# Moving VectorE's share of an RWKV-7 mixer: bonus and gate, filter taps, the tail's order, and throwaway matmuls

## What is computed

```python
def mixer_ab(h, ...):
    # r, k, v, g, a, kk, decay: projections of h, mixed with the token before (r, k, v: 256 x 512)
    y = rwkv7_scan(rh, decay, kh, vh, kk, a)                      # 8 heads of 64
    yc = y - mean(y, -1)                                          # per head
    y = yc * rsqrt(mean(yc * yc, -1) + GN_EPS)
    y = y * lnx_g + lnx_b
    bonus = sum(rh * kh * r_k, -1) * vh                           # per head
    y_a = (y + bonus) * g
    glu = c_val * sigmoid(c_gate)
    conv = depthwise_conv(glu, conv_w, width=31) + conv_b         # 31 taps
    y_b = silu(layer_norm(conv, conv_ln_g, conv_ln_b))
    return concat([y_a, y_b], -1) @ w_out
# around it:  x = x + rms_norm(m, g[3]);  f = swiglu(rms_norm(x, g[4]), ...);  x = x + 0.5 * rms_norm(f, g[5])
```

## Time and profile before

| | |
|---|---|
| median of 3 runs | 2463.41 us (2462.99 to 2463.59) |
| the profiled execution | 2461.77 us |
| its span, first to last instruction | 2460.0 us |
| TensorE busy | 2397.1 us (97%) |
| VectorE busy | 1460.8 us (59%) |
| ScalarE busy | 1071.3 us (44%) |
| GpSimd busy | 121.6 us (5%) |
| TensorE's granted clock, mean | 0.988 of full speed |

### The profile page before, as it was taken

One profiled execution on the slowest core, in us unless ns is written; L12 is line 12 of the kernel. 1 busy time (PEld: TensorE's weight loads), 2 busy tenths in 40 slices (PEclk: granted clock), 3 DMA queues, 4 the chain that ended last, 5 costly groups with the idle time before them and its releaser, 6 DMA issues.

```text
span 2460.0 us, 29664 instructions
## 1 busy us (share of the span) xinstructions
PE 2397.1 (97%) x11572; PEld 1979.5 (80%) x11572; DVE 1460.8 (59%) x1598; ACT 1071.3 (44%) x1308; POOL 121.6 (5%) x145
## 2 busy tenths in 40 slices
PE   8999999999999999999999999998999999999998
PEld 7888877888888888788878887887888888787887
DVE  5445766654654666685455456895545545645544
ACT  4443455444344444554444444423444444545442
POOL 0001000000000100000000002111000000100000
PEclk9999999999999999999999999998999999999999
DMA  8565535565555654355555565204555556343552
GB/s 271 190 218 200 182 103 178 182 205 187 188 188 188 223 186 167 120 205 195 189 188 186 185 220 181 69 1 137 182 190 196 184 188 206 119 141 129 194 187 88
DMA packets 281235, 426.56 MB, mean 173 GB/s; under 512 B 11747, under 2 KB 193635, under 8 KB 281136
## 3 DMA queue, kind: packets, MB, share of 16 engines
q1 hardware_dynamic: 273632, 400.04, 49.1%
q0 software_dynamic: 7520, 25.37, 3.2%
HBM read 422.49 MB, written 1.05 MB: 172 GB/s over the span
## 4 chain that ended last, share of the span: by engine, by line
PE 85%; DVE 11%; ACT 2%; issue 1%; POOL 1%; DMA 0%; SPq 0%; DVEq 0%; POOLq 0%; ACTq 0%
PE bank L1895 25%; PE bank L1897 25%; PE bank L1896 25%; DVE wl L1117 4%; PE bank L2345 2%; PE bank L2037 1%; PE bank L1942 1%; POOL rstd L463 1%; DVE stats L1152 1%; DVE x L1161 1%; PE bank L2140 1%; DVE y L1186 1%; DVE arena L1614 0%; DVE y L1219 0%; PE bank L1949 0%
## 5 line engine op out<-in xcount | busy, mean ns | idle before, releaser
L1117 DVE TENSOR_TENSOR wl<-wf,wh 128x2048 fp32r<-128x2048 f32 x355 | 808.4, 2289 | 419.7 <-ACT wh L622 419.2
L1895 PE MATMUL bank<-wh,xTh 128*128 128x512 f32 x2336 | 929.5, 398 | 16.2 <-DVE wl L1117 7.6
L1897 PE MATMUL bank<-wh,xTl 128*128 128x512 f32 x2336 | 913.4, 391 | 0.0
L1896 PE MATMUL bank<-wl,xTh 128*128 128x512 f32 x2336 | 912.2, 391 | 0.0
L622 ACT ACTIVATE wh<-wf 128x2048 fp32r<-128x2048 f32 x355 | 673.2, 1915 | 250.6 <-PE bank L1897 248.3
L1895 PEld LDWEIGHTS bank<-wh,xTh 128*128 128x128 f32 x2336 | 441.9, 189 | 110.7 <-issue 11.3
L1897 PEld LDWEIGHTS bank<-wh,xTl 128*128 128x128 f32 x2336 | 441.0, 189 | 93.9
L1896 PEld LDWEIGHTS bank<-wl,xTh 128*128 128x128 f32 x2336 | 442.0, 189 | 87.5 <-issue 0.7
L1895 PE MATMUL bank<-wh,hTh 128*128 128x512 f32 x704 | 277.0, 393 | 0.1
L1897 PE MATMUL bank<-wh,hTl 128*128 128x512 f32 x704 | 274.9, 390 | 0.0
L1896 PE MATMUL bank<-wl,hTh 128*128 128x512 f32 x704 | 274.5, 390 | 0.0
(11 more groups left out here) (328 smaller groups left out, 1501.8 us busy)
## 6 DMA issues: line engine op xcount, KB each, us to landing
wf<-in_ffn_w SPq DMA_DIRECT2D x160, 512.0 KB, 4.8
wf<-in_w_in SPq DMA_DIRECT2D x52, 1024.0 KB, 5.4
wf<-in_ffn_w SPq DMA_DIRECT2D x44, 1024.0 KB, 5.0
wf<-in_ffn_w_down SPq DMA_DIRECT2D x44, 1024.0 KB, 5.1
wf<-in_ffn_w_gate SPq DMA_DIRECT2D x80, 512.0 KB, 4.0
wf<-in_ffn_w_up SPq DMA_DIRECT2D x80, 512.0 KB, 4.9
wf<-in_w_branch SPq DMA_DIRECT2D x16, 1024.0 KB, 5.2
wf<-in_c_w_in SPq DMA_DIRECT2D x14, 1024.0 KB, 5.7
```

Source lines behind the costliest of these rows:

```text
L1117: dve.tensor_tensor(wl[s], wf[s], wh[s].bitcast(f32), ALU.subtract).then_inc(SEM[f"lo{s}"], 1)
L1895: pe.matmul(o, lh, rh, start=start, stop=False)
L1896: pe.matmul(o, lh, rl, start=False, stop=False)
L1897: return pe.matmul(o, ll, rh, start=False, stop=stop)
```

## The change

VectorE's sum for the bonus leaves step 8 and comes behind the taps, at step 21, and the products with v and the sum with `lnx_b` are VectorE's own, in steps 22 and 23. POOL's five products are gone; in their place `gated_y` has four operations instead of three: times rstd, times `lnx_g`, plus bonus and `lnx_b`, times g. The last two taps move from steps 22 and 23 to 18 and 20 (`taps_at`). `centred(0)` moves from behind the loop into step 23. In the tail `spread(0)` comes ahead of the convolution's statistics, `centred(1)` and `spread(1)` behind `gated_y(0)`, and TensorE turns half 1 of the convolution only behind the first `part_unit`. In ACT's program `new_square_sum(0)` and `take_x(0)` come ahead of `prep(0, 2)`, and in VectorE's `take_x(0)` ahead of `low(0)`. TensorE gets throwaway products (`busy`), 128x128 by 128x128 into a bank that nobody reads at the time: 12 at the very start, on zeros, before x has landed, 18 behind the turn of x, 14 behind `updates_out`, and 4 behind the first turn of the tail.

```diff
@@ POOL
-        pool.wait_ge(SEM["bonus_done"], c.next("bonus_done"))
-        for b in range(TB):
-            product(heads(r_t[:, b, :]), heads(rv_t[:, b, :]), per_head(bonus[:, 8 * b:8 * b + 8]))
-        product(r_t, r_t, both(lnx_b), ALU.add)
-        product(r_t, r_t, g_t)
-        pool.tensor_tensor(g_t, g_t, both(lnx_g), ALU.mult).then_inc(SEM["post_made"], 1)
+        power(h_rstd[:, 0:8], h_sum[:, 0:8], 8, "head_var", "head_rstd")
         for b in range(TB):
             norm(b)
-        for b in range(TB):
-            power(h_rstd[:, 8 * b:8 * b + 8], h_sum[:, 8 * b:8 * b + 8], 8, "head_var", "head_rstd")
+        power(h_rstd[:, 8:16], h_sum[:, 8:16], 8, "head_var", "head_rstd")
@@ ACT
-        taken(u_s, 1, 4, "u_mm", "u_ready")
...
         y_squares(0)
-        for b in range(TB):
-            silu_conv(b)
+        taken(u_s, 1, 4, "u_mm", "u_ready")
+        silu_conv(0)
+        out_x(0, 1, 6)
+        silu_conv(1)
         y_squares(1)
-        out_x(0, 1, 6)
+        out_x(0, 0, 4)
         out_x(1, 1, 7)
-        out_x(0, 0, 4)
         out_x(1, 0, 5)
...
-        out_of_mixer(RMS)
+        square_sum(0)
+        new_square_sum(0)
+        take_x(0)
+        prep(0, 2)
@@ VectorE
+        dve.memset(sil[:, 0, 0:P], 0.0).then_inc(SEM["zeros"], 1)
...
+        def taps_at(i):
+            if i < 2 or i > 21:
+                return 0
+            return 2 if i > 3 and (i % 2 or i in (18, 20)) else 1
...
-            if i == 8:
-                dve.wait_ge(SEM["rk_made"], c.next("rk_made"))
-                dve.tensor_reduce(bonus, r_t.rearrange("p b (h n) -> p (b h) n", n=HD), X, ALU.add).then_inc(SEM["bonus_done"], 1)
+            if i == 23:
+                centred(0)
             if i == 21:
                 first_state()
-            for _ in range(0 if i < 2 else 2 if i % 2 and i > 3 else 1):
-                if j < CONV:
-                    tap(j)
-                    j += 1
+            for _ in range(taps_at(i)):
+                tap(j)
+                j += 1
+            if i == 21:
...
+                dve.sem_inc(SEM["conv_done"], 1)
+                dve.wait_ge(SEM["rk_made"], c.next("rk_made"))
+                settle(dve.tensor_reduce(bonus, r_t.rearrange("p b (h n) -> p (b h) n", n=HD), X, ALU.add))
+            if i > 21:
+                b = i - 22
+                settle(dve.tensor_tensor(heads(r_t[:, b, :]), heads(rv_t[:, b, :]), per_head(bonus[:, 8 * b:8 * b + 8]), ALU.mult))
+                settle(dve.tensor_tensor(r_t[:, b, :], r_t[:, b, :], lnx_b, ALU.add))
...
-            settle(dve.tensor_tensor(t, t, g_t[:, b, :], ALU.mult))
-            dve.tensor_tensor(t, t, r_t[:, b, :], ALU.add).then_inc(SEM["ya_ready"], 1)
+            settle(dve.tensor_tensor(t, t, lnx_g, ALU.mult))
+            settle(dve.tensor_tensor(t, t, r_t[:, b, :], ALU.add))
+            dve.tensor_tensor(t, t, g_t[:, b, :], ALU.mult).then_inc(SEM["ya_ready"], 1)
@@ TensorE
+        def busy(n, bk, t):
+            for _ in range(n):
+                pe.matmul(bank[bk][:, 0:P], t, t, start=True, stop=True)
...
             turn(1, x, None, (2, 3))
+            busy(18, 0, ident[:, :])
             x_in()
...
+        pe.wait_ge(SEM["zeros"], c.next("zeros"))
+        busy(12, 0, sil[:, 0, 0:P])
         pe.wait_ge(SEM["start_ld"], c.next("start_ld", 16 * 2))
...
-        for b in range(TB):
-            pe.wait_ge(SEM["yb_ready"], c.next("yb_ready"))
-            turn_half(y_conv[:, b, :], 6 + b)
+        busy(14, 1, ident[:, :])
+        pe.wait_ge(SEM["yb_ready"], c.next("yb_ready"))
+        turn_half(y_conv[:, 0, :], 6)
+        busy(4, 1, ident[:, :])
         pe.wait_ge(SEM["ya_ready"], c.next("ya_ready"))
         turn_half(y_rwkv[:, 0, :], 4)
         x_in()
         part_unit(1, 1, 0, 0, True, False)
+        pe.wait_ge(SEM["yb_ready"], c.next("yb_ready"))
+        turn_half(y_conv[:, 1, :], 7)
         part_unit(2, 1, 0, 1, True, False)
```

More of the change, by code:

```diff
@@ L215, in new @@
         names.extend(ns)
-    new("held", "start_ld", "const_ld", "warm", "first_hi", "first_lo", "half", "pre_var", "pre_rstd")
+    new("held", "start_ld", "const_ld", "warm", "zeros", "first_hi", "first_lo", "half", "pre_var", "pre_rstd")
     for s in range(SLOTS):
@@ L232, in program @@
     new("w_mm", "w_ready", "u_mm", "u_ready", "s_mm", "state_in", "y_mm", "yc_ready", "yc_sq", "ya_ready")
-    new("made", "gram_made", "d0_ready", "dt0_mm", "dt0_ready", "rk_made", "bonus_done", "post_made")
+    new("made", "gram_made", "d0_ready", "dt0_mm", "dt0_ready", "rk_made")
     SEM = {n: ctx.enter_context(nc.semaphore(n)) for n in names}
@@ L1643, in take_gram, with centred @@
                    .then_inc(SEM["gram_made"], 1)
+        def centred(b):
+            dve.wait_ge(SEM["y_mm"], c.next("y_mm"))
+            s, o = h_sum[:, 8 * b:8 * b + 8], bank[2 + b][:, :]
+            settle(dve.tensor_reduce(s, heads(o), X, ALU.add))
+            settle(dve.tensor_scalar(s, s, -1.0 / HD, None, ALU.mult))
+            dve.tensor_tensor(heads(y_rwkv[:, b, :]), heads(o), per_head(s), ALU.add).then_inc(SEM["yc_ready"], 1)
         def first_state():
@@ L1677, in _ @@
                 take_gram(i - 2)
-        assert j == CONV
-        dve.wait_ge(SEM["dve"], c.so_far("dve"))
-        dve.sem_inc(SEM["conv_done"], 1)
-        def centred(b):
-            dve.wait_ge(SEM["y_mm"], c.next("y_mm"))
-            s, o = h_sum[:, 8 * b:8 * b + 8], bank[2 + b][:, :]
-            settle(dve.tensor_reduce(s, heads(o), X, ALU.add))
-            settle(dve.tensor_scalar(s, s, -1.0 / HD, None, ALU.mult))
-            dve.tensor_tensor(heads(y_rwkv[:, b, :]), heads(o), per_head(s), ALU.add).then_inc(SEM["yc_ready"], 1)
         def spread(b):
@@ L1713, in out_x @@
                               xTh[:, at[0], at[1]].bitcast(f32), ALU.subtract).then_inc(SEM["xt_ready"], 1)
-        centred(0)
+        spread(0)
         dve.wait_ge(SEM["convT"], c.next("convT", TB))
@@ L1718, in _ @@
             conv_stats(b)
-        spread(0)
         for b in range(TB):
@@ L1723, in _ @@
                .then_inc(SEM["conv_n"], 1)
-        dve.wait_ge(SEM["post_made"], c.next("post_made"))
+        dve.wait_ge(SEM["g_ready"], c.next("g_ready", TB))
+        gated_y(0)
+        out_x(0, 1, 6)
         centred(1)
-        gated_y(0)
         spread(1)
-        out_x(0, 1, 6)
+        out_x(0, 0, 4)
         out_x(1, 1, 7)
-        out_x(0, 0, 4)
         gated_y(1)
@@ L1735, in _ @@
         full = RmsNorm(1.0)
-        out_of_mixer(full)
+        full.variance(0)
+        full.scaled(0)
+        full.pre_variance(0)
+        full.pre_scaled(0)
+        take_x(0)
+        low(0)
         ffn(full, rms, 1.0)
```

2 lines of the change are left out of this document (added).

## The result

| | before | after |
|---|---|---|
| median of 4 runs each | 2463.2 us (2462.79 to 2463.59) | 2440.85 us (2440.11 to 2442.48) |
| profiled execution | 2461.77 us, span 2460.0 | 2440.11 us, span 2438.3 |

The ratio is 0.991 (95% interval 0.9893 to 0.9927): 22.35 us faster between the medians, 21.7 between the two spans.

What follows compares the result with a forecast made beforehand. TensorE is busy 97% of the span, so gains come only from its waits and half clock. Terms -8.3 - 1.65 - 4.8 - 2.6 + 0.5 - 1.4 = -18.25 us give 2445.2 us; range 2442 to 2452.5.

Steps and rivals of the forecast that it cites:

- part 1: Mixer loop, steps 8 to 12: POOL's five products and the r k r_k sum leave; -8.3 us, bounds -6.1 and -8.6.
- Rival (e): Loop: taps are slow for another reason and removing POOL's products gives only 1.2 us; 2452.3 us, chance 0.04.
- GpSimd's power for eight heads: Tail: by the skill page this power should slow VectorE too; the trace shows no such cost and the sum has none.
- parts 2 to 4: Loop's end and tail: sooner taps, late bonus, new order, throwaways, new wait for y_a of half 1; together -1.65 us.
- (a): Tail: the clock falls in the new wait for y_a of half 1, costing 1.7 us; 2446.9 us, chance 0.25.
- (c): Start and tail: throwaways do not keep or wake the clock and run at half speed; 2454.4 us, chance 0.05.
- rival (b): VectorE binds the end of the loop, or its early pairs win less: 3 us, 2448.2 us, chance 0.15.
- just as TensorE wants it: Loop's end: the mask of step 23 ends at 1667.8 us, when TensorE needs it; waiting there was a wrong sign.
- part 5: Seam from mixer to next ffn: earlier squares cut the wait, -4.8 us, half clock gone, -2.6, later hidden tile, +0.5.
- part 6: Start: thirty throwaways wake the clock; gain 1.7 us, cost 0.25, term -1.4 us.
- (d): All 48 throwaways lie on the path at half clock, 22.5 us; 2469.1 us, chance 0.03.
- All the rest, some 2300 us: Everything outside the start, loop steps 8 to 12, mixer tail and seam: same instructions in the same order.

Runs made afterwards that it cites:

- the loop alone: Kernel before with only sooner taps, late bonus on VectorE and gate in new order; old tail and seam orders, no throwaways: 2453.34 us, ratio 0.9965.
- second comparison: Both kernels run once more with no edit: before 2460.93 us, after 2442.43 us, ratio 0.9923 for after.

## Why the prediction was right and where it was wrong

**The loop (part 1, -8.3): right in mechanism, too small by 1.4 us.** That GpSimd's products slow the taps is shown twice: without them the taps take 1.66 us, and with products on a scratch tile 4.57 and 3.11. Rival (e), that the taps are slow for another reason, is out. The step that failed is "8.3 us above 14.94": it took the 7.47 us of the pair from step 6 to step 8 for the floor of the two pairs behind it, and it stopped at step 12. From step 8 to step 10 TensorE's `fill` is shorter and its own pace is 7.20 us, as the test without three taps shows. From step 10 to step 12 TensorE has a group of 32 records (3.84 us instead of 5.62), and VectorE sets the pace at 7.16. And the pairs from step 12 to 14 and from 14 to 16 took 7.47 and 7.15 us before, behind the waits and the half clock; they take 7.14 and 6.69 now, since TensorE comes to them ahead of time. Steps 8 to 12 give 8.9 us (23.24 less 7.19 and 7.16), steps 12 to 18 another 0.8, in all 9.7; the loop alone measured 9.0 in its median. The lower bound of the term, -8.6, was no bound for the same reason.

The Trainium skill (GPSIMD Engine Reference, section 8, Key points) gives the rule by which the two engines contend: an instruction of VectorE in a two-port mode, or with two inputs in SBUF. The trace agrees for the taps with two inputs in SBUF. The first tap has one tensor input and is slowed most (1.14 us instead of 0.34 for one instruction); by the page it would have to be in a two-port mode, which no row shows. The add of 128x1024, with two inputs in SBUF, took 1.53 instead of 1.22, so the price differs by form and the page gives none. The prediction's remark on GpSimd's power for eight heads is borne out in the kernel before, where it lies beside VectorE's normalisation of the convolution, which has two inputs in SBUF (VectorE and GpSimd in order of time):

```profile
1677.93 1.41 DVE L1722 SCALAR_TENSOR_TENSOR arena<-arena,rstd 128x512 f32<-128x512 f32 x2
```

```profile
1678.10 2.08 POOL L463 TENSOR_TENSOR gains<-gains,mhalf 128x8 f32<-128x8 f32 x1 [1.03 <-DVE gains L1693]
```

In the new kernel nothing of GpSimd lies beside the same two instructions, and they take 1.42 us, so VectorE lost nothing; it is the power that is longer, 2.08 us against 1.65 to 1.67 elsewhere in the new mixer. It reads and writes 8 values a partition, the products that slowed VectorE 512 or 1024.

**Sooner taps, late bonus and tail (parts 2 to 4, -1.65): right, 1.4 measured.** From step 18 to the convolution's statistics the new kernel loses 1.25 us (forecast 0.8); the first product came at 1669.43, 8.69 us behind the first statistics where 8.75 was forecast; the new wait for y_a of half 1 was 1.50 us (forecast about 2). That the throwaways keep the clock and that this is worth some 2.5 us is what the test without them says, 2.2, by one trace. What the term did not say: the gain of the order hangs on the clock. With the fall, the turned y_b of half 1 is late, and VectorE's queue with it. Rivals (a) and (c) did not come: no fall behind the waits of 1.23 and 1.50 us. Nor did rival (b): the late masks cost TensorE 1.25 us, not 3. But the mask of step 23, which was to end "just as TensorE wants it", makes 0.4 of that. It is one of the prediction's own signs of being wrong; here it cost little.

**The seam (part 5, -4.8 - 2.6 + 0.5): right.** The turn of x gained 4.8 us between the two traces, and what lies behind it 1.7; the edit alone gave 6.9 us in its median, as the terms say.

**The start (part 6, -1.4): 0.7 in this pair of traces, more over all of them.** The clock stayed up, turns at 0.123 us each and products at 0.23 from the first one on, but x and the weights landed 0.75 and 0.86 us later, which leaves 0.7; the first product came at 13.40, later than the 13 us that the prediction had called a sign of being wrong. One pair does not size this term. VectorE's `xTl` near 199 us, the same instruction in all, stands at 199.18 to 200.96 us in the six traces without the full thirty and at 197.21 to 198.51 in the seven with them, in the median 1.9 us sooner. Rivals (c) and (d) are out: the first product starts 0.14 or 0.15 us behind the low part of its weights with the thirty as without them, so they cost nothing. The term missed what comes with the thirty further on.

**What the range missed.** The step that failed here is "All the rest, some 2300 us, is the same instructions in the same order": it was true, and was taken to mean the same time, a term of nothing. In the two profiled executions the rest differs by two falls of the clock, 1.6 and 1.5 us: 3.1 of the 21.7, and without them the measured time would have been inside the range. Then the traces differ by 18.6, close to the forecast of 18.25, but that is partly luck: the loop's 1.4 too little met 0.4 too much at the start, 0.25 in the tail and 0.4 behind the turn of x. The seven traces with all the throwaways of the start and the six without say that the fall near 396 mostly goes with them, and the one near 1570 comes and goes: the same program had it in one profiled execution and not in the other. The medians say the same in another way: 22.35 us in the first comparison and 19.0 in the second. The range went down 3.2 us below the forecast and held a shorter wait and no late masks; it needed one more term, for clock falls behind waits that the change doesn't touch, some 1.5 us each, of both signs. In the second comparison the new kernel's median, 2442.43 us, lies inside the range.

## What to carry to other kernels

A floor read from one iteration holds only for iterations with the same work: count the records of each group before a time per step is carried over. GpSimd's products of 512 and more values a partition were paid for by VectorE here, with no semaphore between the two, so look for such work where VectorE is idle or works from PSUM. Small throwaway products in a wait cost nothing where the wait was longer than they are, and were worth some 2 us where half clock would have delayed a tile that VectorE's queue stood behind. A term for the start, or for a fall of the clock, wants several traces of each kernel: one pair gave 0.7 us where thirteen traces give 1.9.

## What the runs showed of the hardware that was not expected

- The same wait of TensorE, 1.84 us near 396 and 1.87 near 1570, is followed by half clock in one execution and not in another, at a cost of 1.5 to 1.6 us. The waits of about 0.35, 1.23 and 1.5 us in the tail were followed by no fall in any of the seven traces that have the new tail with its throwaways. The Trainium skill (TensorE: Matmul & The Clock Gate, Part 1: The HAM clock gate) says that the chip's look at activity runs free of the kernel, so that the same kernel's slow stretch differs between runs. The two traces of the kernel before agree: half clock from 13.6 to 17.0 us in one, products at half speed from 12.9 to 18.9 in the other.
- With thirty throwaways in the first 13 us the clock fell near 396 us in one of seven traces, without all of them in six of six, each time 378.9 us behind the start's half clock. That is a count and a distance, not a cause.
- The kernel before ranges over 7 us from run to run (2456.49 to 2463.8 in 24 runs), and four runs that agree within 0.8 us, as in the first comparison, did not show it.
